# A gated linear recurrence with mirrored tiles: two tiles share one stationary operand

## What is computed

```python
q = silu(u @ w_q); f = lb + (1 - lb) * sigmoid(u @ w_f); k = 1 - f; i = u @ w_i; gate = silu(u @ w_g)
S_t = diag(f_t) S_{t-1} + k_t i_t^T          # state, 128 x 128
o_t = S_t^T q_t
out = h + (rms_norm(o) * gate) @ w_out       # u is the normed h
```

## Time and profile before

| what | value |
|---|---|
| median of 3 runs | 1313.38 us (1313.25 to 1313.77) |
| span of the profiled execution | 1312.2 us, 21253 instructions |
| its own time against the median | span 1.2 us shorter |
| TensorE matmul busy | 1249.1 us, 95% |
| VectorE, ScalarE, GpSimd busy | 776.4, 413.4, 186.7 us |
| second layer's projections | from about 670 to 1182 us of the span |

### The profile page before, as it was taken

One profiled execution on the slowest core, in us unless ns is written; L12 is line 12 of the kernel. 1 busy time (PEld: TensorE's weight loads), 2 busy tenths in 40 slices (PEclk: granted clock), 3 DMA queues, 4 the chain that ended last, 5 costly groups with the idle time before them and its releaser, 6 DMA issues. The chain is left out here.

```text
span 1312.2 us, 21253 instructions
## 1 busy us (share of the span) xinstructions
PE 1249.1 (95%) x7872; PEld 1145.4 (87%) x7872; DVE 776.4 (59%) x1520; ACT 413.4 (32%) x872; POOL 186.7 (14%) x354
## 2 busy tenths in 40 slices
PE   6999999999999999499989999999999999995998
PEld 5999999999999998378869898989898989895887
DVE  5657575656666665934435575756575757568421
ACT  4544444444444444412221212121222222214200
POOL 2321212121212121500030000000000000005100
PEclk9999999999999999799989999999999999996999
DMA  7210303020203020335521102020202020203352
GB/s 224 73 42 1 81 1 81 0 80 0 80 0 82 13 69 17 92 106 172 160 67 47 33 1 81 2 80 1 82 1 81 1 81 1 81 1 109 111 166 96
DMA packets 96518, 81.94 MB, mean 62 GB/s; under 512 B 5040, under 2 KB 86960, under 8 KB 96432
## 3 DMA queue, kind: packets, MB, share of 16 engines
q1 hardware_dynamic: 96432, 80.76, 20.7%
HBM read 63.97 MB, written 16.78 MB: 62 GB/s over the span
## 5 line engine op out<-in xcount | busy, mean ns | idle before, releaser
L28 PE MATMUL p_proj<-w_qkv_hi,ut_hi 128*128 128x384 f32 x512 | 175.6, 343 | 5.4 <-DVE w_qkv_lo L494 4.5
L30 PE MATMUL p_proj<-w_qkv_hi,ut_lo 128*128 128x384 f32 x512 | 172.2, 336 | 0.0
L29 PE MATMUL p_proj<-w_qkv_lo,ut_hi 128*128 128x384 f32 x512 | 171.9, 336 | 0.0
L28 PE MATMUL p_proj<-g_w_ig_hi,next_hi 128*128 128x256 f32 x512 | 147.0, 287 | 0.0
L30 PE MATMUL p_proj<-g_w_ig_hi,next_lo 128*128 128x256 f32 x512 | 144.6, 282 | 0.0
L29 PE MATMUL p_proj<-g_w_ig_lo,next_hi 128*128 128x256 f32 x512 | 143.9, 281 | 0.0
L28 PE MATMUL p_proj<-next_hi,w_qf_hi 128*128 128x512 f32 x320 | 129.3, 404 | 3.5 <-issue 1.8
L30 PE MATMUL p_proj<-next_hi,w_qf_lo 128*128 128x512 f32 x320 | 126.2, 394 | 0.0
L29 PE MATMUL p_proj<-next_lo,w_qf_hi 128*128 128x512 f32 x320 | 126.1, 394 | 0.0
L554 DVE TENSOR_TENSOR_SCAN a_skip<-a_skip 128x128 f32<-128x128 f32 (+3 forms) x64 | 93.6, 1462 | 33.0 <-ACT a_beta L416 32.3
L28 PEld LDWEIGHTS p_proj<-w_qkv_hi,ut_hi 128*128 128x128 f32 x512 | 96.7, 189 | 6.6 <-issue 4.9
(11 more groups left out here) (186 smaller groups left out, 2766.7 us busy)
## 6 DMA issues: line engine op xcount, KB each, us to landing
stage<-in_sb_w_in_dram SPq DMA_DIRECT2D x32, 512.0 KB, 5.8
stage<-in_hg_w_in_dram SPq DMA_DIRECT2D x32, 512.0 KB, 4.5
m_in<-mixed_scratch SPq DMA_DIRECT2D x12, 512.0 KB, 5.7
a_beta<-in_x_dram SPq DMA_DIRECT2D x8, 512.0 KB, 3.9
mixed_scratch<-a_gated SPq DMA_DIRECT2D x8, 512.0 KB, 3.3
stage<-in_sb_w_out_dram SPq DMA_DIRECT2D x8, 512.0 KB, 4.2
l_h_tile<-in_x_dram SPq DMA_DIRECT2D x8, 512.0 KB, 3.7
h_scratch<-l_h_tile SPq DMA_DIRECT2D x8, 512.0 KB, 5.0
```

Source lines behind the costliest of these rows:

```text
L28: pe.matmul(out, w_hi, m_hi, start=start, stop=False, skip_group_check=True)
L29: pe.matmul(out, w_hi, m_lo, start=False, stop=False, skip_group_check=True)
L30: return pe.matmul(out, w_lo, m_hi, start=False, stop=stop, skip_group_check=True)
```

## The change

In the second layer tiles 4 to 7 hold their 128 tokens in reverse order: the copies out of the transposes write them so, and the last copy of each head turns them back. In a reversed tile the left half of a block lies at its right. So the left halves of tile m and of tile m + 4 fill complementary columns: `k_left` shrinks from 1024 to 512 columns, all used, and one matmul has 128 stationary columns (64 of either tile) and 2 x 64 moving columns (of either tile's `q_right`), written to two places of the bank 256 columns apart. Four matmuls take the place of eight in each level, the last included. VectorE's operations reach both kinds of tiles with patterns of three dimensions. The masks become 512 columns wide, for six levels, and are made for the two kinds of tiles apart. The last level is copied in two pieces.

The diff, cut:

```diff
+MIRRORED_FROM = TILES // 2
...
-            "level_mask": sb("level_mask", [P, len(LEVELS), P // 2]),
...
+def in_tile_order(t, tile):
+
+    return t[:, :, ::-1] if tile >= MIRRORED_FROM else t[:, :, :]
...
+def lefts(t, half):
+
+    whole = t[:, :]
+    return bass.AP(tensor=whole.tensor, offset=whole.offset,
+                   ap=[whole.ap[0], [HALF + half, 2], [2 * half, HALF // (2 * half)], [1, half]])
...
+def rights(t, half):
+
+    whole = t[:, :]
+    return bass.AP(tensor=whole.tensor, offset=whole.offset + half,
+                   ap=[whole.ap[0], [HALF - half, 2], [2 * half, HALF // (2 * half)], [1, half]])
...
+def shared_lefts(t, half):
+
+    whole = t[:, :]
+    return bass.AP(tensor=whole.tensor, offset=whole.offset,
+                   ap=[whole.ap[0], [half, 2], [2 * half, HALF // (2 * half)], [1, half]])
...
+def tile_end(m):
+
+    return m * P + (0 if m >= MIRRORED_FROM else P - 1)
...
                         act.activation(ut_hi[:, 4 * half:4 * half + 4, j * P:(j + 1) * P],
-                                       turned[half][:, :, :], ACT.Copy).then_inc(hi_ready, 1)
+                                       in_tile_order(turned[half], j), ACT.Copy).then_inc(hi_ready, 1)
...
-                        dve.tensor_tensor(ut_lo[:, 4 * half:4 * half + 4, j * P:(j + 1) * P], turned[half][:, :, :],
+                        dve.tensor_tensor(ut_lo[:, 4 * half:4 * half + 4, j * P:(j + 1) * P],
+                                          in_tile_order(turned[half], j),
...
-        k_left = [sb(f"k_left{i}", [P, SEQ]) for i in range(2)]
-        scores = [sb(f"scores{b}", [P, TILES, P]) for b in range(2)]
+        k_left = [sb(f"k_left{i}", [P, HALVES]) for i in range(2)]
+        score_rows = [sb(f"scores{b}", [P, SEQ]) for b in range(2)]
+        level_mask = sb("level_mask", [P, MASKED, HALF])
+        scores = [rows[:, :].rearrange("p (m t) -> p m t", m=TILES) for rows in score_rows]
...
-                act.activation(scores[b][0:P // 2, :, P // 2:P],
-                               level_bank(L - 1, projects)[0:P // 2, :].rearrange("p (m t) -> p m t", m=TILES),
+                bank = level_bank(L - 1, projects)[:, :].rearrange("p (m t) -> p m t", m=TILES)
+                early, late = slice(0, MIRRORED_FROM), slice(MIRRORED_FROM, TILES)
+                act.activation(scores[b][0:P // 2, early, P // 2:P], bank[0:P // 2, early, :], ACT.Copy)
+                act.activation(scores[b][P // 2:P, late, 0:P // 2], bank[P // 2:P, late, :],
                                ACT.Copy).then_inc(last_placed, 1)
...
-                            act.activation(out_turned[:, u * HALF:(u + 1) * HALF],
-                                           p_misc[2 + u][:, :, :].rearrange("p a b -> p (a b)"), ACT.Copy,
+                            act.activation(out_turned[:, u * HALF:(u + 1) * HALF].rearrange("p (a b) -> p a b", b=P),
+                                           in_tile_order(p_misc[2 + u], 4 * u), ACT.Copy,
...
-                k_out = by_halves(k_left[level % 2], half)[:, :, 0, :]
-                k_in = by_halves(k[b], half)[:, :, 0, :]
+                k_out = shared_lefts(k_left[level % 2], half)
+                k_in = lefts(k[b], half)
...
-                    dve.tensor_tensor(k_out, k_in, suf[:, :, 0, :], ALU.mult).then_inc(k_prepared, 1)
+                    dve.tensor_tensor(k_out, k_in, lefts(suf, half), ALU.mult).then_inc(k_prepared, 1)
                     dve.wait_ge(doubled, 2 * (L * h + level))
-                dve.tensor_tensor(q_out, by_halves(q[b], half)[:, :, 1, :], pre[:, :, 1, :],
+                dve.tensor_tensor(q_out, rights(q[b], half), rights(pre, half),
                                   ALU.mult).then_inc(prepared, 1)
...
-                dve.tensor_tensor(pre[:, :, 1, :], pre[:, :, 1, :],
-                                  pre[:, :, 0, half - 1:half].to_broadcast([P, blocks, half]),
+                dve.tensor_tensor(rights(pre, half), rights(pre, half), left_ends(pre, half),
...
-                dve.wait_ge(masks_made, 1 + 2 * L)
-                dst = scores[b][:, :, :].rearrange("p m (b two r) -> p m b two r", two=2, r=half)[:, :, :, 1, :]
-                mask = c["level_mask"][:, level, :].bitcast(I32).rearrange("p (b r) -> p b r", r=half)
-                dve.copy_predicated(dst, mask.unsqueeze(1).to_broadcast([P, TILES, blocks, half]),
-                                    bank[:, :].rearrange("p (m b r) -> p m b r", m=TILES, r=half)
+                dve.wait_ge(masks_made, 1 + 4 * MASKED)
+                mask = level_mask[:, level, :].bitcast(I32).rearrange("p (e b r) -> p e b r", e=2, r=half)
+                dve.copy_predicated(rights(score_rows[b], half), mask,
+                                    bank[:, :].rearrange("p (e b r) -> p e b r", e=2, r=half)
...
-                pool.memset(k_left[i][:, :], 0.0).then_inc(zeroed, 1)
-
-                pool.memset(scores[i][:, :, :], 0.0).then_inc(zeroed, 1)
-            pool.memset(c["level_mask"][:, :, :], 1.0).then_inc(masks_made, 1)
+                pool.memset(score_rows[i][:, :], 0.0).then_inc(zeroed, 1)
+            pool.memset(level_mask[:, :, :], 1.0).then_inc(masks_made, 1)
             pool.wait_ge(masks_made, 1)
...
+            for n, half in enumerate(LEVELS[:MASKED]):
+                for e in range(2):
+
+                    mask = level_mask[:, n, e * HALF // 2:(e + 1) * HALF // 2]
+                    mask = mask.rearrange("p (m b r) -> p m b r", m=TILES // 2, r=half)
+                    pool.affine_select(out=mask, in_=mask, compare_op=ALU.is_ge, fill=0.0, base=-e * half,
+                                       pattern=[[0, TILES // 2], [-2 * half, P // 2 // half], [0, half]],
+                                       channel_multiplier=1).then_inc(masks_made, 1)
...
-                rows = P if level < L - 1 else P // 2
-                for m in range(TILES):
-                    last = pe.matmul(level_bank(level, projects)[0:rows, m * (P // 2):(m + 1) * (P // 2)],
-                                     k_left[level % 2][:, m * P:m * P + rows],
-                                     q_right[level % 2][:, m * (P // 2):(m + 1) * (P // 2)], start=True, stop=True)
+                bank = level_bank(level, projects)[:, :].rearrange("p (e m t) -> p e m t", e=2, m=TILES // 2)
+                right = q_right[level % 2][:, :].rearrange("p (e m t) -> p e m t", e=2, m=TILES // 2)
+                for m in range(TILES // 2):
+                    last = pe.matmul(bank[:, :, m, :], k_left[level % 2][:, m * P:(m + 1) * P], right[:, :, m, :],
+                                     start=True, stop=True)
```

More of the change, by code:

```diff
@@ L130, in start_output_tile, with left_ends, right_ends @@
                          w_hi[:, h, cols], w_lo[:, h, cols], h == 0, False)
+def in_tile_order(t, tile):
[8 more added lines that the diff above has]
+                   ap=[whole.ap[0], [HALF - half, 2], [2 * half, HALF // (2 * half)], [1, half]])
+def left_ends(t, half):
+    whole = t[:, :]
+    return bass.AP(tensor=whole.tensor, offset=whole.offset + half - 1,
+                   ap=[whole.ap[0], [HALF + 1, 2], [2 * half, HALF // (2 * half)], [0, half]])
+def right_ends(t, half):
+    whole = t[:, :]
+    return bass.AP(tensor=whole.tensor, offset=whole.offset + 2 * half - 1,
+                   ap=[whole.ap[0], [HALF - (2 * half - 1), 2], [2 * half, HALF // (2 * half)], [0, half]])
+def shared_lefts(t, half):
+    whole = t[:, :]
+    return bass.AP(tensor=whole.tensor, offset=whole.offset,
+                   ap=[whole.ap[0], [half, 2], [2 * half, HALF // (2 * half)], [1, half]])
+def tile_end(m):
+    return m * P + (0 if m >= MIRRORED_FROM else P - 1)
 def load_columns(sp, stage, w_in, h, p):
@@ L1333, in split_lo @@
                 dve.tensor_tensor(lo, stage[p][:, :, :], hi.bitcast(F32), ALU.subtract).then_inc(w_ready[p], 1)
-            def by_halves(t, half):
-                return t[:, :].rearrange("p (b two r) -> p b two r", two=2, r=half)
             def prepare(h, b, level):
                 half = LEVELS[level]
-                blocks = SEQ // (2 * half)
-                pre, suf = by_halves(prefix[b], half), by_halves(suffix, half)
+                pre, suf = prefix[b], suffix
                 if level == 0:
@@ L1346, in prepare @@
                     if known_first(h):
-                        dve.wait_ge(zeroed, 5)
+                        dve.wait_ge(zeroed, 3)
                     else:
@@ L1356, in prepare @@
                     dve.wait_ge(level_done, L * h)
-                q_out = q_right[level % 2][:, :].rearrange("p (b r) -> p b r", r=half)
-                k_out = by_halves(k_left[level % 2], half)[:, :, 0, :]
-                k_in = by_halves(k[b], half)[:, :, 0, :]
+                q_out = q_right[level % 2][:, :].rearrange("p (e b r) -> p e b r", e=2, r=half)
+                k_out = shared_lefts(k_left[level % 2], half)
+                k_in = lefts(k[b], half)
                 if level == 0:
@@ L1368, in prepare @@
```

(18 more changed lines are left out.)

11 lines of the change are left out of this document (1 added, 10 removed).

## The result

The changed kernel takes 1271.03 us (median of 4 runs, 1270.04 to 1274.35) against 1313.32 us (1311.83 to 1313.77) for the kernel before: a ratio of 0.9686, 95% interval 0.9672 to 0.9699 (the medians alone give 0.9678). The forecast was 1274 us, with a range of 1271 to 1286. The execution that was profiled is the longest of the four: 1274.35 us, with a span of 1272.6.

A forecast was written before the change was run, and what follows sets the result against it. TensorE was taken to bound the kernel from first to last projection: 45 x 0.844 + 7 x 0.19 = 39.3 us off the profiled 1312.2 gives 1272.9, with 1.2 us to the median 1274 us; range 1271 to 1286.

The forecast's parts named there:

- The pitch of a full record: TensorE's levels: a record with 128 moving columns and a full stationary operand costs 110.7 ns, 8 records 0.886 us.
- the cover of 0.91 us ahead of the transposes: VectorE's gating ends before TensorE's transposes of the outputs: 2.63 us ahead before, 0.94 forecast to be left, no wait.
- the reversed reads: ScalarE's and VectorE's copies with negative steps: taken as zero, at most 1.6 us if at half speed.
- the shapes on VectorE: VectorE's level operations get three free dimensions instead of two: no change taken, bounds 0.6 us either way on an operation.
- ScalarE's two copies: ScalarE's last placement as two copies of 256 elements: some 0.2 us more per head, counted as zero.
- The first rival: VectorE's chain ahead of the transposes grows by over 0.94 us and TensorE waits for it: 1289 us, chance 0.09.
- The second and third: Rivals on TensorE's levels: split operand's jump slows records, 1297 us, chance 0.03; records no longer overlap, 1343 us, chance 0.05.
- A level of 0 to 5: On TensorE, each goes from 1.73 to 0.886 us and saves 0.844; 45 such levels counted.
- Level 6: TensorE's last level, 64 stationary columns before: from 1.08 to 0.886 us, saving 0.19, counted seven times.
- 0.5 us either way: Tail: GpSimd starting 0.84 us earlier may catch one more VectorE operation and free another, 0.5 us gained or lost.
- the sentence that VectorE may be held beside the selections: First head: VectorE's two-input operations may be held beside GpSimd's mask selections, by one selection each; only short ones left at 697.
- The cover of 5.5 us that the forecast counted on: GpSimd's masks end near 699, before VectorE's first predicated copy at 704.55: cost zero, 2.3 us lost once at most.

The follow-up runs named there:

- the second experiment: Changed kernel with each level's four matmuls reading and writing one run of 128 columns instead of 2 x 64 with a jump: 1272.33 us, ratio 0.9677.
- the first experiment: Changed kernel with eight matmuls a level again, each stationary operand loaded once for each of its two tiles: 1318.85 us, ratio 1.0032.
- the fourth experiment: Changed kernel with GpSimd making every mask selection twice and the copies waiting for the second: 1293.22 us, ratio 0.9837.
- the third experiment: Changed kernel with the stationary operand of each level matmul cut from 128 to 64 columns: 1286.57 us, ratio 0.9786.

## Why the prediction was right, and which terms were off

**The forecast's mechanism held.** The pitch of a full record (0.111 us measured, 0.1107 taken), the count of 8 a level, TensorE as the bound of the heads, the cover of 0.91 us ahead of the transposes (0.94), the reversed reads, the shapes on VectorE and ScalarE's two copies (all zero) came as worked out. The first rival needed VectorE's chain to grow by 0.94 us; it did not grow. The second and third needed a price for the jump; the second experiment shows none.

**The heads saved 5.67 us each, not 5.25.** Two terms were mis-sized.
- A level of 0 to 5 saved 0.89 us, not 0.844. The forecast took the 1.73 us of a level with 128-column matmuls behind it, and there it held: 1.73 - 0.89 = 0.84. But three of the six stand ahead of a projection, where one takes 1.70 us with the old records (as in the first experiment) and 0.81 or 0.80 with the new: the handing over is 0.08 to 0.09 shorter for the new records and 0.03 for the old ones, so 0.90 is saved.
- Level 6 saved 0.35 us (5.67 less six times 0.886), not 0.19. The rows show it too: from the projection's last record ahead of it to the projection behind it, it took 811.64 - 810.25 = 1.39 us, and a level now takes 909.59 - 908.56 = 1.03. The forecast set the length of its records against eight new ones of 0.111 us and no more. Of what it missed, 0.09 us is the later start (0.32 instead of 0.23), which went with the change of the operand's width, and 0.08 the shorter handing over of the new level.

**The sum by place.** By the starts of the key transposes of neighbouring heads and of the last level 3 (1181.96 and 1140.30), both profiled executions give: 7.04 us by head 0 (0.74 of it before the layer, see GpSimd's first clear at 669.40 against 670.14, and none of the change's doing; 5.67 as in other heads; 0.6 not explained), 31.94 in heads 1 to 6, 2.68 in the last three levels, 41.66 in all where the forecast had 39.3. Six heads at 5.67 would be 34.0; the missing 2.1 are the branch, which cost the head that holds it 2.0 us before and 4.0 after.

**What the profiled execution lost again.** From 41.66 us at the last level 3, 39.6 are left at the end of the span. That this is nearly the 39.3 of the forecast is luck: larger savings and the 0.74 us ahead of the layer made up for the branch and for what follows. VectorE's chain in the tail accounts for 0.2 of it: the key transposes, the first work behind that chain, come 41.46 us earlier. GpSimd's splits caught one more operation (1144.73, 2.85 us) and let another go, as the prediction had it, 0.5 us either way. The next 0.87 us lie between the column sums and the transposes of the outputs, where TensorE is busy throughout and the mean granted clock is 0.77 instead of 0.81; the last 1.0 us lie behind the last matmul. Nothing in the change accounts for either, nor for the branch's 2 us, and the other three runs are 2.8 to 4.3 us shorter; as they were not traced, it is not shown that they lack just these. The forecast's 1274 us stands 3 us above the median, which is what a saving a head that is 0.42 us too small gives in seven heads (2.9 us).

**The masks ended later than forecast**, at 703.63 instead of 699, though GpSimd began 0.74 us earlier. A finest selection takes the 2.12 us that were worked out (2.13), and the fill 2.66. What failed is the sentence that VectorE may be held beside the selections, by one selection each, which leaves GpSimd its pace: the selections stretched too. A selection whose like took 2.12 us at 674.81 took 3.16 at 679.09, and a level multiply on VectorE took 0.95 us at 697.11 instead of 0.68. The cover of 5.5 us that the forecast counted on was 1.25, and the fourth experiment shows what lies behind it.

## What to carry to other kernels

Where TensorE bounds a stretch and its matmuls move fewer columns than they load, count the loads: two tiles behind one stationary operand halve them, and here the price for reordering tokens so that they can share was nothing. Check each piece of cover that shortens with the faster engine, for what is hidden by 1 us is one size away from 20 us. And once the bound engine's stretch is shorter, look at what was always outside it: a wait of one line in the tail and a loop written out gave another 0.7%.

## What the hardware showed that was not expected

- A change between 64 and 128 columns of the stationary operand, there and back, costs TensorE 0.30 to 0.33 us (61.82 and 64.34 us a head against 59.69). A narrow operand that loads in less time (136 ns a record in the third experiment instead of 191) made the kernel slower, at ratios of 0.9786 and 0.9939 against 0.9686.
- The idle time at the loop's branch had an echo: the changed kernel was idle for 2.17 us, and from 902 to 906 us the granted clock was 0.62, near the 1.2 GHz level, which cost nearly 2 us more. Both were gone where the loop was written out. In the kernel before the stall was 1.8 us, its head only 2.0 us longer than the others, and the clock behind the stall stayed at 1.00. Of the eight profiled executions with the branch, five were idle there for 1.43 to 1.94 us, and their heads are 1.7 to 2.2 us longer than the others; three (the changed kernel, the one run of columns, the masks made twice) were idle for 2.17 to 2.28 us, and theirs are 4.0 to 4.2 us longer, with clocks of 0.62 to 0.65 behind the stall. So the fall came with the longer stalls; why a stall is longer in one execution than in another stays open.
- GpSimd's selections and VectorE's work stretch each other in the first head (3.16 for 2.12 us, 0.95 for 0.68). In the tail VectorE's multiplies take 2.85 us beside GpSimd's splits and 0.68 where GpSimd is held back.
